# A transpose of the identity ahead of projection chunks and of the turns of the FFN loops

## The reference

```
for li in range(2):
    x = x + 0.5 * swiglu(rmsnorm(x), ffn_w_in[li, 0], ffn_w_out[li, 0])
    x = x + (hgrn2_mixer or mla_mixer)(rmsnorm(x))
    x = x + 0.5 * swiglu(rmsnorm(x), ffn_w_in[li, 1], ffn_w_out[li, 1])
    x = x + sigmoid(rmsnorm(x) @ ple_w_gate[li]) * (p[li] @ ple_w_in[li])
x = rmsnorm(x)
for l in range(2):
    h = rmsnorm(x) * (1 + scale) + shift
    x = x + gate * rmsnorm(hybrid_mixer(h, w_in[l], w_out[l], ...))
```

## Time and profile before

| what | value |
|---|---|
| median of three runs | 1525.78 us (1515.85, 1525.78, 1534.03) |
| profiled execution, its own time | 1533.64 us |
| its span, first to last instruction | 1531.8 us |
| mean granted clock of TensorE | 0.992 of 2.4 GHz |
| busy: TensorE matmuls, DVE, ACT, POOL | 97%, 71%, 50%, 11% |
| read from HBM | 262.44 MB, 172 GB/s over the span |

### The profile page before, as it was taken

One profiled execution on the slowest core, in us unless ns is written; L12 is line 12 of the kernel. 1 busy time (PEld: TensorE's weight loads), 2 busy tenths in 40 slices (PEclk: granted clock), 3 DMA queues, 4 the chain that ended last, 5 costly groups with the idle time before them and its releaser, 6 DMA issues.

```text
span 1531.8 us, 31078 instructions
## 1 busy us (share of the span) xinstructions
PE 1490.0 (97%) x12389; PEld 1436.8 (94%) x12389; DVE 1085.9 (71%) x1571; ACT 764.5 (50%) x1154; POOL 173.4 (11%) x218
## 2 busy tenths in 40 slices
PE   6999999999999999999999999999999999999998
PEld 6999999989999999999998989999998997789968
DVE  5877567996887568877657665697568867486582
ACT  5544455455544446544445264554346436454382
POOL 1110011721240110101010000211100100010000
PEclk9999999999999999999999999999999999999999
DMA  6876745243786655776555235586654754047400
GB/s 211 265 238 222 259 138 166 77 143 97 242 266 218 212 168 178 239 245 216 192 167 157 85 110 165 181 286 225 212 167 138 225 155 120 2 118 240 142 1 28
DMA packets 218796, 264.86 MB, mean 173 GB/s; under 512 B 22253, under 2 KB 196301, under 8 KB 218701
## 3 DMA queue, kind: packets, MB, share of 16 engines
q1 hardware_dynamic: 208728, 234.64, 49.2%
q0 software_dynamic: 8960, 27.37, 5.3%
q10 hardware_dynamic: 1013, 1.52, 0.3%
HBM read 262.44 MB, written 1.05 MB: 172 GB/s over the span
## 4 chain that ended last, share of the span: by engine, by line
PE 83%; DVE 10%; ACT 4%; DMA 2%; issue 1%; POOL 0%; DVEq 0%; SPq 0%; ACTq 0%
PE twin L1098 24%; PE twin L1100 24%; PE twin L1099 24%; DVE w_lo L1835 3%; PE twin L1513 1%; PE twin L1753 1%; PE twin L1715 1%; PE twin L1527 1%; PE twin L1525 1%; PE twin L1123 1%; DVE hg_s L2070 1%; ACT w_hi L695 1%; DVE hg_f L2052 1%; PE twin L1112 1%; DVE hg_f L2051 1%
## 5 line engine op out<-in xcount | busy, mean ns | idle before, releaser
L695 ACT ACTIVATE w_hi<-w_raw 128x1024 fp32r<-128x1024 f32 (+1 forms) x452 | 453.4, 1037 | 442.2 <-PE twin L1100 280.3
L1098 PE MATMUL twin<-xh,w_lo 128*128 128x256 f32 x2312 | 654.9, 283 | 10.6 <-ACT X L705 3.5
L1835 DVE TENSOR_TENSOR w_lo<-w_raw,w_hi 128x1024 fp32r<-128x1024 f32 (+1 forms) x452 | 547.8, 1248 | 143.6 <-ACT w_hi L695 142.4
L1100 PE MATMUL twin<-xh,w_hi 128*128 128x256 f32 x2312 | 649.2, 281 | 0.0
L1099 PE MATMUL twin<-xl,w_hi 128*128 128x256 f32 x2312 | 649.2, 281 | 0.0
L1098 PEld LDWEIGHTS twin<-xh,w_lo 128*128 128x128 f32 x2312 | 437.6, 189 | 14.8 <-issue 8.7
L1099 PEld LDWEIGHTS twin<-xl,w_hi 128*128 128x128 f32 x2312 | 438.8, 190 | 1.6 <-issue 1.2
L1100 PEld LDWEIGHTS twin<-xh,w_hi 128*128 128x128 f32 x2312 | 436.8, 189 | 0.2
L1098 PE MATMUL twin<-hh,w_lo 128*128 (+1 forms) x704 | 196.4, 279 | 0.0
L1099 PE MATMUL twin<-hl,w_hi 128*128 (+1 forms) x704 | 196.1, 279 | 0.0
L1100 PE MATMUL twin<-hh,w_hi 128*128 (+1 forms) x704 | 196.1, 279 | 0.0
(11 more groups left out here) (377 smaller groups left out, 2002.1 us busy)
## 6 DMA issues: line engine op xcount, KB each, us to landing
w_raw<-in_ffn_w_in SPq DMA_DIRECT2D x176, 512.0 KB, 4.7
w_raw<-in_ffn_w_out SPq DMA_DIRECT2D x88, 512.0 KB, 4.3
w_raw<-in_w_in SPq DMA_DIRECT2D x52, 512.0 KB, 4.7
mod_raw<-in_w_ada POOLq DMA_DIRECT2D x128, 192.0 KB, 4.4
w_raw<-in_a_w_in SPq DMA_DIRECT2D x32, 512.0 KB, 4.4
w_raw<-in_ple_w_gate SPq DMA_DIRECT2D x16, 512.0 KB, 4.5
w_raw<-in_b_w_out SPq DMA_DIRECT2D x16, 512.0 KB, 3.7
w_raw<-in_w_out SPq DMA_DIRECT2D x16, 512.0 KB, 4.5
```

The source lines that it names most:

```text
L695: A(w_hi[:, c % NSLOT, cols], w_raw[:, c % NRAW, cols], ACT.Copy).then_inc(*did(hi_ready))
L1098: mm(out, lhs[1], rhs[0], start=start, stop=False, skip_group_check=skip)
L1100: return mm(out, lhs[0], rhs[0], start=False, stop=stop, skip_group_check=skip)
L1835: V.tensor_tensor(w_lo[:, c % NSLOT, cols], w_raw[:, c % NRAW, cols], f32(w_hi[:, c % NSLOT, cols]), ALU.subtract).then_inc(*did(lo_ready))
```

## The change

A new helper `in_step(b)` issues one transpose of the identity, with the identity also as the other operand, into the first 128 columns of bank b. Nobody reads the result; the next matmul to that place begins a new accumulation. The helper is called

- in `columns`, when `waits` is None, between the wait for the chunk and its matmuls
- in the loop of `ffn`, once a turn, ahead of the turn's first gate chunk
- ahead of the out part of each `ffn` in bank 4, and, except in f = 2, at the begin of each turn of its loop in bank 3, which is taken first
- in `bout`, ahead of q = 2 and q = 5, in bank 4, which is taken first

```diff
--- before.py
+++ after.py
@@ -1093,6 +1093,10 @@
             for _ in range(n):
                 mm(bank[7][:, 0:T], ones[:, :], const[:, 0:T], start=True, stop=True)
 
+        def in_step(b):
+
+            nc.tensor.transpose(bank[b][:, 0:P], ident, ident)
+
         def three(out, lhs, rhs, start, stop, skip=False):
 
             mm(out, lhs[1], rhs[0], start=start, stop=False, skip_group_check=skip)
@@ -1140,6 +1144,8 @@
 
             take(b)
             pe.wait_ge(lo_ready, 2 * (c + 1))
+            if waits is None:
+                in_step(b)
             w = split(c, (kd, width))
             if waits is not None:
                 last = as_they_come(b, w, waits, xs)
@@ -1212,6 +1218,8 @@
                     p = 1 + j
                     b = 2 * (p % 2)
                     pe.wait_ge(gate_scaled, n0 + p + 2 * it)
+                    if j == 0:
+                        in_step(b)
                     half(c + 2 + 2 * j, b, False, it).then_inc(*did(pe_groups))
                     pe.wait_ge(up_scaled, n0 + p + 2 * it)
                     half(c + 3 + 2 * j, b + 1, False, it).then_inc(*did(pe_groups))
@@ -1226,6 +1234,9 @@
             c = first[f"out{f}"]
             for b in range(4, 8):
                 take(b)
+            if f != 2:
+                take(3)
+            in_step(4)
 
             def rows(c, q, it=None, only=None):
                 pe.wait_ge(lo_ready, 2 * (c + 1) + (0 if it is None else 8 * it))
@@ -1244,6 +1255,8 @@
             for q in range(2):
                 rows(c + q, q).then_inc(*did(pe_groups, ("chunk", c + q)))
             with pe.Fori(0, 2) as it:
+                if f != 2:
+                    in_step(3)
                 for q in range(4):
                     rows(c + 2 + q, 2 + q, it).then_inc(*did(pe_groups))
             start = at[("chunk", c + 1)][1]
@@ -1576,7 +1589,10 @@
             transposes(("b", i), sB[:, i % 3])
         bout(1)
         values_b(7)
+        take(4)
         for q in range(2, 8):
+            if q in (2, 5):
+                in_step(4)
             bout(q)
         at[("chunk", c0 + 7)] = at[("bout", 3)]
         for m in range(4):
```

## The result

The changed kernel takes 1540.03 us (median of 17 runs, 1535.47 to 1545.33), the kernel before 1524.18 us (median of 17, 1514.20 to 1534.11). The ratio is 1.0106, 95% interval 1.0087 to 1.0125: slower by about 1%, where a small gain was forecast. The runs spread over 10 us, half of the 20 us of before. The profiled execution took 1539.42 us, 5.8 more than the profiled one of before.

The account below looks back on a forecast made before the run. TensorE's matmul pitch, with two paces (113.3 and 117.7 ns), was taken to bound the kernel. From the profiled 1533.6: -26.6 pace, +10.3 transposes, +1.3 bout gave 1519 us; range 1510 to 1541, the forecast's own 1512 to 1523.

Parts of the forecast that it names:

- why a transpose should choose the fast pace: At 75 places, one transpose makes following matmuls run at 113.3 instead of 117.7 ns: -26.6 us.
- DVE's cover: DVE and DMA keep up with TensorE at the quicker pace; late w_lo costed at nothing, at most 1 or 2 us.
- the loop from 32 to 218: Stretch from 32 to 218 us of the profile, counted as an in loop at 117.7 ns, expected at 113.3.
- The two new waits: take(3) ahead of the out stages and take(4) in bout, costed at nothing since those banks are long free.
- The price of a transpose: Each of 75 transposes costs TensorE 0.137 us, together +10.3 us.
- the two bounds: Cost of one transpose: 0.137 us against a fast flow, 0.106 against a slow one.
- rival (b): One transpose locks the slow pace for all 8980 matmuls behind transposes: 1555 us; chance 0.11.
- Bout: In bout, q 2 to 7, matmuls fast now turn slow behind the transposes: +1.3 us.
- (a): Each transpose draws the pace by chance: 1517.3 + 39.5 s us for slow share s, 1531 in the middle; chance 0.25.
- (c): Transposes leave the pace unchanged, only their cost remains: 1542 us from the profile, 1534 from the median; chance 0.07.
- (d): Matmuls behind transposes keep a pace quicker than 113.3 ns: 1480 us; chance 0.05, shared with a far cheaper transpose.
- The spread: Runs 18 us apart explained by the two paces; a spread far under 18 us would support that.

Follow-up runs that it names:

- The narrow matmul: The changed kernel with a float32 matmul of one column instead of the transpose at each of the 75 places: 1551.29 us.
- the kernel of 1519.48: Kernel before with sums moved into each FFN's first up chunk, four transposes ahead of each in loop and the f = 2 out part: 1519.48 us, ratio 0.9969.

## Why the prediction was wrong

**The step that failed** is "why a transpose should choose the fast pace". The prediction said itself that all its places had four or six transposes in a row, "that one does the same isn't shown", and then took it for all. Six of seven rows of four or six were read as a property of the transpose, but one, two and three in a row do something else than four: behind a quick flow 25 of 39, 11 of 24 and 20 of 22 places went slow, and none of 49 with four. With four 24 us of the forecast gain appeared (8845 matmuls quick), with one 1.2 us. A row of six wasn't run.

**What bounds the kernel**: right. No wait changed its place, DVE's cover held (with four in a row and most matmuls quick, TensorE waits 2.6 us for w_lo ahead of the transposes, and 3.2 us with one), and the time lost or won is TensorE's pitch and the transposes themselves. What the prediction calls the loop from 32 to 218 is the in loop and the out part of the first FFN; its sum counts both. The two new waits, costed at nothing, show no cost: the 3.2 us of idle time ahead of the transposes all end with DVE's w_lo, which is the wait for the chunk that was there before.

**The price of a transpose**: 0.114 us measured in place of the 0.137 taken, 8.6 us and not 10.3. It lay between the two bounds (0.106 and 0.137). The two bounds were sound: over nine distances, the pace taken off, a transpose costs 0.134 us where the flow is quick ahead and behind (median of 7 places) and 0.115 where it is slow (26 places). The forecast took the dearer one because it set all matmuls quick, and most were slow. The 0.114 of rival (b) is what the first two matmuls behind it show. The Trainium skill (TensorE: Matmul & The Clock Gate, Part 4: PE-mode transpose) gives a duration of about 275 ns, and the trace agrees with 272; as time lost it would be more than twice too much.

**Bout**, forecast slow behind both transposes, went half that way: its matmuls stayed quick behind the one at 923 us and turned slow behind the one at 940 us (rows of 276 and 281 ns with `ol` moving), about 0.6 us of the 1.3.

**The sum**: 1533.6 - 26.6 + 10.3 + 1.3 becomes 1533.6 - 1.2 + 8.6 = 1541.0. The term that is off by 25 us is the gain.

**The point of departure.** To subtract from the long profiled execution of 1533.6 was sound only if the change settled the pace. As it didn't, the median of before was the thing to beat, and it holds some 2100 fewer slow matmuls. A change that gains nothing by pace then costs 8.6 us, and this one has some 1850 more slow by the estimate above.

**The rivals.** (a), a draw at each transpose, gave nearly the right time: its 1517.3 + 39.5 s with the share of 46 in 73 places that were slow behind, s = 0.63, is 1542. Its mechanism is wrong: the result differs from place to place, but repeats in 60 of 72 and, where the flow ahead was alike, in 56 of 59. So its good time is luck: it left the slow share open. (b), one transpose locks the slow pace, holds behind a quick flow that the transpose meets at 115 ns, and not elsewhere. (c), nothing changes the pace, had 1542 from the profile, as near, by luck too: the turns of the loop exclude it, and the matmuls that turned quick and slow nearly cancel (1.2 us). The narrow matmul is the one that behaves so. (d), a pace under 113.3, is in no long stretch measured. The Trainium skill's 109.2 ns (same page, Back-to-back issue gap) is not reached in any long stretch of any of the eight offsets; the page gives that formula for single matmuls in isolation, not for pairs with a weight load as here, and the prediction left that out.

**The spread** of the runs fell from 20 to 10 us, as the prediction wanted for its explanation, though the gain didn't come. The second execution of before shows one cause of the spread: with 2292 fewer slow matmuls it is 12.8 us shorter. A likely reason for the narrower one is that the pace now changes at 75 places instead of being handed on through long stretches, so that a run is nearer to its mean; no run tests this.

**Open:** whether the moment of the restart selects the pace, and by what; why the placement of operands sets what the paces are; why one transpose out of a slow flow gives either; why four fail behind float32 sums (3 of 4) and failed once behind `three` (at 954 us in the kernel of 1519.48).

## What to carry to other kernels

When the same instructions run at two pitches, look first at what stands exactly at the places where the pitch changed, and copy all of it, its number too: one instruction of a kind isn't the row of four that was seen. A profiled execution at the edge of the spread is no base for a sum unless the change removes the spread; count the paces in a second trace of the kernel before. And if a pace persists, pay for it once ahead of the long loop, not at each turn: 75 rows of four gave 24 us and cost 33, five rows cost about 2 and left a gain of 3 at best.

## What the runs showed of the hardware

- A dense flow of 128x256 fp32r matmuls had a pitch of 113.3 to 119.9 ns with the clock at 1.00 throughout, by the offset of its operands; eight offsets moved the kernel from 1521 to 1566 us, five of them in one execution each.
- At one offset two pitches are stable, 113.3 ns for 1538 matmuls on end and 117.7 for 1582, and an interruption of one, two, three or four transposes leads from one to the other in a way that doesn't grow with the number. The same place with the same pace ahead gave the same result in 56 of 59 cases.
- A first transpose costs 0.115 us in a slow flow and 0.134 in a quick one, and each further one 0.11, at a row duration of 272 ns.
- A float32 matmul of a single column costs more than the transpose of 128 columns, 0.225 us by the time of the kernel and by the timeline.
